# One encoder layer on one core: group A's key sums taken a unit later, turned maxima next to the following scores, group B's first buffers apart from A's last

## The reference

```python
n = _rmsnorm(h, attn_norm[i])
proj = n @ w_in[i]
qa, ka, va, qb, kb, vb = jnp.split(proj, splits, axis=-1)
qa = _axial_rope(_rmsnorm(qa, q_norm_a[i]), tables)   # 8 query heads
ka = _axial_rope(_rmsnorm(ka, k_norm_a[i]), tables)   # 2 key/value heads
out_a = _gqa_blocked(qa, ka, va)                      # full softmax attention, group A
out_b = _neighbourhood_attention(qb, kb, vb, rpb_b[i])  # 8 x 16 window, learned bias, group B
mixed = jnp.concatenate([_rmsnorm(out_a, out_norm_a[i]), _rmsnorm(out_b, out_norm_b[i])], axis=-1)
h = h + mixed @ w_out[i]
...
h = h + (a * jax.nn.gelu(g, approximate=True)) @ w_down[i]
...
return _rmsnorm(h, final_norm)
```

## Time and profile before

| what | value |
|---|---|
| time, median of 3 runs | 2118.94 us (2118.48 to 2120.27) |
| the profiled execution | 2117.14 us, its span 2115.40 us |
| busy share of the span | PE 97%, PEld 77%, DVE 62%, ACT 39%, POOL 22% |
| granted TensorE clock, mean | 0.988 |

### The profile page before, as it was taken

One profiled execution on the slowest core, in us unless ns is written; L12 is line 12 of the kernel. 1 busy time (PEld: TensorE's weight loads), 2 busy tenths in 40 slices (PEclk: granted clock), 3 DMA queues, 4 the chain that ended last, 5 costly groups with the idle time before them and its releaser, 6 DMA issues.

```text
span 2115.4 us, 28952 instructions
## 1 busy us (share of the span) xinstructions
PE 2043.1 (97%) x9990; PEld 1625.1 (77%) x9990; DVE 1315.1 (62%) x1777; ACT 823.9 (39%) x1361; POOL 459.8 (22%) x323
## 2 busy tenths in 40 slices
PE   8999998999989999999999999999999999999996
PEld 6788886555567788788888888888888888787885
DVE  6799735888866766796655665566553544434546
ACT  6323112444456741254433443333432433423223
POOL 4122204555522134201221122112200100102101
PEclk9999999999999999999999999999999999999998
DMA  5233447211068432202111211121147544341103
GB/s 184 76 133 119 164 154 188 49 45 45 1 142 184 100 150 99 90 13 82 50 64 64 68 48 63 64 69 59 50 177 244 183 145 161 111 146 45 40 30 120
DMA packets 82689, 212.64 MB, mean 101 GB/s; under 512 B 26561, under 2 KB 26945, under 8 KB 82625
## 3 DMA queue, kind: packets, MB, share of 16 engines
q1 hardware_dynamic: 81760, 210.70, 31.6%
q10 hardware_dynamic: 864, 1.13, 0.1%
HBM read 156.75 MB, written 55.05 MB: 100 GB/s over the span
## 4 chain that ended last, share of the span: by engine, by line
PE 75%; DVE 9%; issue 7%; POOL 3%; DMA 2%; ACT 2%; SPq 1%; POOLq 0%; DVEq 0%; ACTq 0%
PE ps L320 23%; PE ps L322 23%; PE ps L321 23%; POOL key_sum L1111 2%; DVE qstd L736 1%; DMA KLB<-qkl 1%; PE ps L1263 1%; DVE qt L749 1%; PE ps L1239 1%; PE ps L1173 1%; PE ps L1156 1%; PE ps L1202 1%; DVE nmax L1417 1%; DVE H L2614 0%; SPq L935 0%
## 5 line engine op out<-in xcount | busy, mean ns | idle before, releaser
L320 PE MATMUL ps<-NH,WH 128*128 128x512 f32 x840 | 334.3, 398 | 17.2 <-DVE WL L719 8.9
L321 PE MATMUL ps<-NL,WH 128*128 128x512 f32 x840 | 330.6, 394 | 0.0
L322 PE MATMUL ps<-NH,WL 128*128 128x512 f32 x840 | 330.5, 393 | 0.0
L320 PE MATMUL ps<-NL,NH 128*128 128x512 f32 x528 | 206.7, 391 | 3.6 <-ACT tok_std L1544 3.4
L322 PE MATMUL ps<-NL 128*128 128x512 f32 x528 | 206.1, 390 | 0.0
L321 PE MATMUL ps<-NH 128*128 128x512 f32 x528 | 206.1, 390 | 0.0
L320 PE MATMUL ps<-NH,AH 128*128 128x512 f32 x528 | 205.4, 389 | 0.0
L321 PE MATMUL ps<-NL,AH 128*128 128x512 f32 x528 | 205.4, 389 | 0.0
L322 PE MATMUL ps<-NH,AL 128*128 128x512 f32 x528 | 205.4, 389 | 0.0
L2391 DVE TENSOR_TENSOR NL<-raw,NH 128x1024 fp32r<-128x1024 f32 x66 | 81.8, 1240 | 197.5 <-ACT NH L2245 197.5
L320 PEld LDWEIGHTS ps<-NH,WH 128*128 128x128 f32 x840 | 160.0, 190 | 54.8 <-DVE NL L713 8.9
(11 more groups left out here) (253 smaller groups left out, 4072.1 us busy)
## 6 DMA issues: line engine op xcount, KB each, us to landing
raw<-in_w SPq DMA_DIRECT2D x102, 512.0 KB, 3.4
A_raw<-in_wu SPq DMA_DIRECT2D x84, 256.0 KB, 2.6
act<-ca SPq DMA_DIRECT2D x22, 768.0 KB, 3.3
NH<-act SPq DMA_DIRECT2D x66, 256.0 KB, 3.5
xst<-in_xT SPq DMA_DIRECT2D x24, 256.0 KB, 3.4
H<-in_xT SPq DMA_DIRECT2D x8, 768.0 KB, 8.9
H<-hT SPq DMA_DIRECT2D x8, 768.0 KB, 6.4
out_yT<-H SPq DMA_DIRECT2D x24, 256.0 KB, 2.1
```

The lines of the kernel that those rows point to most:

```text
L320: nc.tensor.matmul(out, wh, xh, start=first, stop=False, skip_group_check=onto)
L321: nc.tensor.matmul(out, wh, xl, start=False, stop=False, skip_group_check=onto)
L322: return nc.tensor.matmul(out, wl, xh, start=False, stop=last, skip_group_check=onto)
```

## The change

It moves instructions, and adds none but the register work of their waits. On TensorE `score_block` is split into `first_pass` and `second_pass`. A unit now begins with the first passes of blocks 0 and 1 and the first max pass, then both second passes (in a short unit another max pass), then the other blocks as before. The sums by `blk` are those of the unit before and stand between the last max pass and the values (`sums`). `max_rows` stands behind all values and writes to bank 2 (`ROW_BANK`). In front of the first unit TensorE waits for two of GpSimd's memsets, not for six; the order of these is changed. Behind group A, `PF` and four of the `VF` blocks lie in the first half of `PT`, each `VF` block is a tensor of its own, `key_sum` and `key_part` lie outside of `PT`. ScalarE's wait for the last sums is gone; the last sums (TensorE) and the last `out` (VectorE) stand in step 1 of group B, and a `square` moves from step 3 to step 1.

```diff
@@ buffers
+        VF = [nc.alloc_sbuf_tensor_at(f"VF{n}", [P, len(NA_LEFT), P], F32, offset=probs_home + (6 + 2 * n + 2 * (n > 2)) * KB) for n in range(VBLOCKS)]
         lows_home = c.at
-        VF = c("VF", [VBLOCKS, len(NA_LEFT), P])
         c = Region(lows_home + 16 * KB)
-        key_sum, key_part = over("key_sum", c.at, [2, GT], F32), over("key_part", c.at, [2, GT], F32, 4 * KB)
-        PR = c("PR", [2, TS])
+        key_sum, key_part = c("key_sum", [2, GT]), c("key_part", [GT])
+        PR = c("PR", [2, 3 * P])
@@ s2_pool
-            for n, (v, value) in enumerate(((KL["A"][0][one_row, :], 1.0), (KL["A"][1][one_row, :], 1.0), (blk[:], 1.0), (neg1[:], -1.0),
+            for n, (v, value) in enumerate(((KL["A"][0][one_row, :], 1.0), (blk[:], 1.0), (KL["A"][1][one_row, :], 1.0), (neg1[:], -1.0),
@@ s2_tensor
-            def score_block(p, b, kb):
+            def first_pass(p, b, kb):
                 s, g = divmod(b, 3)
                 k = window("A", 4 * b)[0] + kb * P
                 pe.wait_ge(a_exp, blocks_before(p, b) + (kb + 1))
...
+            def second_pass(p, b, kb):
...
                 if kb == 0:
                     pe.wait_ge(row_ok, p * 6 + (b + 1))
...
+            def sums(p, b):
+                bank = ps[:, UNIT_BANK[b % 2], :]
+                pe.wait_ge(d_sum, p * 12 + (2 * b + 2))
+                for half in range(2):
+                    mm = nc.tensor.matmul(bank[cols(half, DH), HALF_Q:GT], blk[:, 0:DH], key_sum[:, b % 2, cols(half, HALF_Q)],
+                                          start=True, stop=True)
+                mm.then_inc(pv_done, 1)
 
             def phase(p, b, before, after):
                 n = UNIT_BLOCKS[b]
                 s = b // 3
-                for kb in range(n):
-                    score_block(p, b, kb)
+
+                def another(t):
+                    if after:
+                        max_pass(*after, t)
+                    elif t < 2:
+                        scores_b(NPAIR_A, t)
+
+                first_pass(p, b, 0)
+                first_pass(p, b, 1)
+                another(0)
+                second_pass(p, b, 0)
+                second_pass(p, b, 1)
+                if n == 4:
+                    another(1)
+                for kb in range(2, n):
+                    first_pass(p, b, kb)
+                    second_pass(p, b, kb)
                     if kb % 2 == 1:
-                        for t in ((kb - 1, kb) if n == 4 else (kb // 2,)):
...
+                        for t in (2, 3) if n == 4 else (kb // 2,):
+                            another(t)
                 bank = ps[:, UNIT_BANK[b % 2], :]
+                if before:
+                    if isinstance(p, int) and (p, b) == (0, 1):
+                        pe.wait_ge(zeroed, 6)
+                    sums(*before)
                 pe.wait_ge(o_done, p * 6 + (b + 1))
                 for kb in range(n):
...
-                    if kb == n - 2 and after:
-                        max_rows(*after)
-                pe.wait_ge(d_sum, p * 12 + (2 * b + 2))
...
+                if after:
+                    max_rows(*after)
@@ step of s2_tensor
+                if before == "A" and m == 1:
+                    sums(p - 1, 5)
...
-            pe.wait_ge(zeroed, 6)
+            pe.wait_ge(zeroed, 2)
@@ s2_scalar
+                if m == 1 and before == "A":
+                    square(p - 1, 1)
                 if m == 3:
-                    if before == "A":
-                        square(p - 1, 1)
                     square(p - 1, 2)
...
-            act.wait_ge(pv_done, NPAIR_A * 6)
@@ s2_vector
+                if before == "A" and m == 1:
+                    out("A", p - 1, 5)
...
-            out("A", NPAIR_A - 1, 5)
             every_pair(dve, step)
```

More of the change, by code:

```diff
@@ L862, in build @@
         HALF_Q = GT // 2
-        UNIT_BANK = (6, 7)
+        UNIT_BANK, ROW_BANK = (6, 7), 2
         def blocks_before(p, b):
@@ L981, in value_part @@
         def value_part(block):
-            return flat(VF[:, block, :, :]), ps[:, VBANK, :]
+            return flat(VF[block][:]), ps[:, VBANK, :]
         def read_out(kind, p, m, before, middle):
@@ L1200, in score_block @@
                 pe.wait_ge(a_exp, blocks_before(p, b) + (kb + 1))
-                out = ps[:, 4 + kb % 2, :]
-                nc.tensor.matmul(out, KH["A"][s][:, k:k + P].bitcast(F32R), QS["A"][s][:, cols(g)].bitcast(F32R), start=True, stop=False)
+                nc.tensor.matmul(ps[:, 4 + kb % 2, :], KH["A"][s][:, k:k + P].bitcast(F32R), QS["A"][s][:, cols(g)].bitcast(F32R),
+                                 start=True, stop=False)
+            def second_pass(p, b, kb):
+                s, g = divmod(b, 3)
+                k = window("A", 4 * b)[0] + kb * P
                 if kb == 0:
                     pe.wait_ge(row_ok, p * 6 + (b + 1))
-                nc.tensor.matmul(out, KL["A"][s][0:DH + 1, k:k + P].bitcast(F32R), Q2A[s][0:DH + 1, cols(g)].bitcast(F32R),
+                nc.tensor.matmul(ps[:, 4 + kb % 2, :], KL["A"][s][0:DH + 1, k:k + P].bitcast(F32R), Q2A[s][0:DH + 1, cols(g)].bitcast(F32R),
                                  start=False, stop=True).then_inc(st_rdy, 1)
+            def sums(p, b):
[5 more added lines that the diff above has]
+                mm.then_inc(pv_done, 1)
             def phase(p, b, before, after):
@@ L1225, in phase @@
                                          PT[:, b % 2, kb, cols(half, HALF_Q)], start=kb == 0, stop=kb == n - 1)
-                    if kb == n - 2 and after:
-                        max_rows(*after)
-                pe.wait_ge(d_sum, p * 12 + (2 * b + 2))
-                for half in range(2):
-                    mm = nc.tensor.matmul(bank[cols(half, DH), HALF_Q:GT], blk[:, 0:DH], key_sum[:, b % 2, cols(half, HALF_Q)],
-                                          start=True, stop=True)
-                mm.then_inc(pv_done, 1)
+                if after:
+                    max_rows(*after)
             def turn(kind, p, m):
@@ L1258, in weigh_both @@
                 if m % 4 == 0:
-                    pe.wait_ge(o_done, p * 6 + b - 1 + (before == "A" and m == 0) + O_FREE)
+                    pe.wait_ge(o_done, p * 6 + b - 1 + O_FREE)
                 first, w = window("B", m)
@@ L1262, in weigh_both @@
                     for half in range(2):
-                        mm = nc.tensor.matmul(ps[cols(half, DH), PVBANK_B[b % 2], cols((m // 2) % 2, P)], VF[0:kn, first + kb, (m + half) % 4, cols(s, DH)],
+                        mm = nc.tensor.matmul(ps[cols(half, DH), PVBANK_B[b % 2], cols((m // 2) % 2, P)], VF[first + kb][0:kn, (m + half) % 4, cols(s, DH)],
                                               PF[0:kn, (m // 2) % 2, kb, cols(half, P)],
@@ L1344, in row_copy @@
                 act.wait_ge(row_t, p * 6 + (b + 1))
-                nc.scalar.activation(Q2A[s][DH:DH + 1, cols(g)].bitcast(F32R), ps[DH:DH + 1, 0, :], ACT.Copy, scale=-1.0).then_inc(row_ok, 1)
+                nc.scalar.activation(Q2A[s][DH:DH + 1, cols(g)].bitcast(F32R), ps[DH:DH + 1, ROW_BANK, :], ACT.Copy, scale=-1.0).then_inc(row_ok, 1)
             def squares(p, b):
@@ L1472, in phase @@
                 dve.wait_ge(a_exp, done)
-                nc.vector.tensor_tensor(key_part[:, b % 2, :], PT[:, b % 2, n - 2, :], PT[:, b % 2, n - 1, :], ALU.add).then_inc(d_sum, 1)
+                nc.vector.tensor_tensor(key_part[:], PT[:, b % 2, n - 2, :], PT[:, b % 2, n - 1, :], ALU.add).then_inc(d_sum, 1)
                 dve.wait_ge(d_sum, p * 12 + (2 * b + 1))
                 dve.wait_ge(p_sum, p * POOL_SUMS + (FIRST_SUM[b] + n - 3))
-                nc.vector.tensor_tensor(key_sum[:, b % 2, :], key_sum[:, b % 2, :], key_part[:, b % 2, :], ALU.add).then_inc(d_sum, 1)
+                nc.vector.tensor_tensor(key_sum[:, b % 2, :], key_sum[:, b % 2, :], key_part[:], ALU.add).then_inc(d_sum, 1)
                 if before:
```

6 lines of the change are left out of this document (1 added, 5 removed).

## The result

The changed kernel takes 2110.01 us (median of 6 runs, 2104.97 to 2112.92), the kernel before on the same chip 2120.57 (6 runs, 2118.48 to 2125.08): ratio 0.9946, 95% interval 0.9935 to 0.9958, that is 8.9 to 13.8 us less. Two later comparisons gave 0.9954 (0.9939 to 0.9969) and 0.9957 (0.9945 to 0.9969). The forecast of 2114.0 us had the direction right, and the time lies within its range, but the gain came out at about twice the 4.9 us forecast (10.56 us between the medians).

What follows compares the result with a forecast made beforehand. TensorE, busy in 97% of the span, was taken as the bound. The terms summed as -1.4 - 0.9 + 1.3 + 0.5 - 2.7 - 1.7 = -4.9 us, from 2118.94 to 2114.0 us, range 2109.5 to 2119.0.

Steps and rivals of the forecast that it cites:

- term 1: Start of group A's units: the second pass of block 0 comes later, costing long units +0.63 or +0.5 us each.
- term 4: First units: block 2 starts behind the first exponential, -1.4 us; the unit behind it falls to 11.3 us, -0.9.
- terms 1 to 3: Group A's steady part: +2.0 + 3.5 - 4.2 = +1.3 us, within its error no change.
- Term 2: Long units before long ones: sums leave the path; units of 11.48 us should take 11.3; long units together +2.0 and +3.5.
- Term 3: Short units: gain 0.8 us each, less 0.35 in four where GpSimd also adds a square; -4.2 us in all.
- Term 5: Group A's end: +0.5 us for the late start, -2.7 for the moved `out`, -1.7 for the moved square.
- the signs: List of what traces would show, among them VectorE's first group B maximum 3 us earlier and GpSimd's first add 0.5 later.
- the rival of gains given back: Group A's end: VectorE's moved `out` delays item 4, another wait replaces the square's, 1.3 of 4.4 us left; chance 0.25.
- The rival of the holes: Units: GpSimd pays for meeting VectorE, short units lose 0.7 to 1.4 us each, 2119.5 to 2124.4 us; chance 0.12.

Runs made afterwards that it cites:

- rows_back: The changed kernel with the turned maxima back ahead of the last block's values, new order of passes kept; 2113.46 us, ratio 0.9969 to the kernel before.
- start_only: The kernel before with only the new order of the memsets and the wait for two of them; 2118.08 us (one run; before 2119.27).
- rows_early: The changed kernel with both the turned maxima's place and the order of passes put back; 2105.96 us, ratio 0.9936 to the kernel before; its copy 2104.60 us.
- a_only: The changed kernel with group A's end as before, new buffers and order inside units kept; 2115.11 us, ratio 0.9981 to the kernel before.
- b_only: The kernel before with group A's end alone changed, last sums in their old place; 2113.66 us, ratio 0.9973 to the kernel before.
- order_back: The changed kernel with the old order of passes at a unit's start, turned maxima still behind all values; 2109.93 us, ratio 0.9962 to the kernel before.
- square_back: The changed kernel with both squares of group A's end in step 3 again; 2110.19 us (one run).

## Why the prediction was right in its direction and wrong in its size

The miss of 3.9 us (8.8 in the stretches against 4.9) lies in two steps: a unit's tail was left at its old length (2.5 us in units 2 to 23, term 1), and the first unit was priced as if its exponentials and its tail stayed (1.6 us, term 4).

**Term 1, the unit's start, held; the length built on it did not.** Forecast for block 2's first pass: 2.13 and 1.90 us into the unit. Measured 2.11 and 2.11; before a short unit the second pass was held by the row copy, at 0.93 us instead of 0.81; with the row early (`rows_back`) it stood at 0.80 and block 2 at 1.88. The step that failed is the next one, "should take 10.67 + 0.63 = 11.3": it left the unit's tail at its old length. The change takes the turning out from between the values, so that TensorE goes once less from one kind of matmul to another. From start to start, the turning took 0.58 us with values behind it (in `start_only`, whose units are those of before) and takes 0.40 with first passes behind it; the last block's values 0.48 behind the turning and 0.39 among the others; the sums 0.53 at the unit's end and 0.48 ahead of values. Together that is the 0.33 us of 4.77 against 4.44, to 0.01. `rows_back` is the test: with the old tail the long units last 11.35 and 10.88 us (forecast 11.3 and 10.9), and its 21 units behind the second 224.21 - 11.35 = 212.86 us against 223.90 - 12.23 = 211.67 before, +1.2 where terms 1 to 3 said +1.3 (by kinds of unit +2.4, +3.1 and -4.3, forecast +2.0, +3.5 and -4.2). With the new tail the 21 units take 221.92 - 11.04 = 210.88, -0.8. Only long units before a long one keep the 0.3. Before a short one most of it goes to the late row (block 2 at 2.11 instead of 1.88). In a short unit nothing is left (8.11 in both kernels): its sums begin 5.40 us into it instead of 5.08, as it begins earlier against VectorE's maxima.

**Term 2 held.** No wait for `key_sum` is left, and the units with a square fell from 11.48 to 11.11 us (11.3 forecast, and 11.35 in `rows_back`).

**Term 3 held in its size, in part by luck.** Short units gave -3.8 in all, forecast -4.2; the three with b = 0 last 8.11 us, the four with b = 3 last 8.25 to 8.46, forecast 8.0 and 8.35. But the reason given for the 0.35, a square that GpSimd adds in four of them, is not there: in the trace of before, squares are added in the three with b = 0. The slower four follow a unit in which GpSimd's second add begins 4.20 to 4.33 us in, not 3.99. GpSimd's second add begins 3.99 us into a long unit (445.28 - 441.29) where it began after 3.30 (458.60 - 455.30): 0.7 later, as the first one is, forecast 0.5.

**Term 4 was too small, by 1.6 us.** I wrote that the first exponentials "started at 344.50 behind SP's signal", "and that stays". It did not stay: they come 7.49 us behind the first max pass after, 7.30 in `start_only`, 8.21 before. The trace of before names SP as the last to release them, but in the second profile of before it names TensorE's second pass, 8.20 us behind the first max pass too. So SP's signal does not come at a fixed time, and TensorE's late second pass at the low clock was the holder, or nearly level with it. In all eleven profiles with the new start SP is named, 7.3 to 7.8 us behind the first max pass. In the three of the changed kernel this gives 0.6 us. The rest is the first unit's tail: its sums, 0.58 us from their start to the next unit's in both profiles of before, are now in the second unit, and term 4 didn't count that. `start_only` with its old tail lasts 14.00 us, `rows_early` and its copy, which differ from it there mainly by the sums' place, 13.45 and 13.35, all three with the granted clock up in this unit. The clock adds its scatter: 12.7 to 14.7 us over all profiles with the new start. The second unit lasts 11.03 instead of 12.23, -1.2 for -0.9: the tail again.

**Term 5 held in its sum (-3.8 for -3.9), not in its shares; that is luck.** The late start costs 1.4 there (`a_only` against before), forecast 0.5; the edits of the end give 53.07 - 47.91 = 5.2 (`a_only` against the changed kernel), forecast 4.4. Without the new units they give 3.5 (`b_only`). Of the 5.2, 4.15 are stops of TensorE: 1.69 for `key_sum`, 2.94 for `VF` and 1.73 for the square, of which 2.21 for `VF` are left. The square alone is worth about 1.0, not 1.7. The rest, 1 us, may be the shorter stretch of low clock; no run settles it. VectorE's maximum of group B's item 2, the first behind the `out`, came 14.48 us behind the last unit's start instead of 16.48: 2 us earlier, forecast 2.7 (3 among the signs). The other 0.7 is the last `key_sum`, which began that much later in the unit (10.21 us, 9.51 before), forecast 0.5. Its item 4 had no idle time left, as the rival of gains given back has it, but its lateness reached nobody that the waits show; only in `b_only` did something of the kind occur, by the keys.

**The rival of the holes did not occur.** GpSimd's 64 adds into `key_sum` last 1.286 us at the median (1.285 before), at most 1.81 (1.78 before), 87.6 us in all in both kernels. In the meeting at group A's end it is VectorE that pays: its last `key_sum` took 1.67 us beside GpSimd's add of a square (582.83), 0.693 at the median; it did so before, too (1.66). The Trainium skill's page "SBUF — State Buffer", section "SBUF: two separate sides", has such a pair lock each other out for a whole instruction, whichever starts first; the trace agrees in that the 0.98 us more are most of the add's 1.27, and shows VectorE, which began second, as the one that pays here.

## What to carry to other kernels

When an instruction moves, price both places: the one it goes to, and the neighbours that meet where it stood, since a step on TensorE can cost more or less by what stands beside it (here one change of kind of matmul less came with 0.33 us a unit). Where an instruction waits for two things, to remove one can show nothing; try both at once before the place is called harmless or lost, as `rows_early` shows against `order_back` and `rows_back`. A releaser named for a wait is the last one in that execution only: before "that stays" is written, look at a second profile, or at what the other sources of the wait were doing.

## What the runs showed of the hardware beyond that

The stretch in which TensorE is granted the lower clock after an idle time starts and ends elsewhere from one execution to the next with the same waits ahead of it: in the first unit of the changed kernel it lies between 338 and 346 us in one profile, between 345 and 350 in two, and the first unit's length differs by 1.2 us with it. In `square_back`, whose first unit is the same, the clock stayed at 1.00 there (12.72 us) and through group B's first lap after a stop of 2.2 us behind which the three profiles of the changed kernel show 0.50. A single profile's sum of such a place is good to about 1 us only.
